# Expert outputs added to the residual by one indirect transfer of whole rows per expert, in place of three of quarter rows

## The reference, cut to what matters

```python
top_v, top_i = lax.top_k(logits, TOP_K)            # 4 of 32 experts for each of 512 tokens
top_w = jax.nn.softmax(top_v, axis=-1)
...
gu = xb @ w_gate_up[e] + b_gate_up[e]              # rows of expert e, 1024 -> 2048
gate = jnp.minimum(gu[:, :D_EXPERT], SWIGLU_LIMIT)
up = jnp.clip(gu[:, D_EXPERT:], -SWIGLU_LIMIT, SWIGLU_LIMIT)
glu = gate * jax.nn.sigmoid(SWIGLU_ALPHA * gate)
return ((up + 1.0) * glu) @ w_down[e] + b_down[e]  # 1024 -> 1024
...
y = jnp.zeros((t + 1, d), out.dtype).at[row_tok].add(out * row_w[:, None])
```

## Time and profile before

| | |
|---|---|
| median of 3 runs | 2087.03 us (2084.79 to 2087.28) |
| profiled execution: span, first to last instruction | 2083.6 us |
| TensorE busy, of the span | 2054.8 us, 99% |
| VectorE, ScalarE, GpSimd busy | 862.4, 455.5, 369.3 us |
| read from HBM, written to it | 509.09 MB, 18.88 MB |
| granted TensorE clock, mean | 0.999 |

### The profile page before, as it was taken

How to read it: one execution, slowest core, us unless ns; L and a number is a source line. 1 busy time by engine, 2 the same in 40 slices (tenths; PEclk the granted TensorE clock), 3 DMA queues, 4 the chain that set the end, 5 groups by cost and what they waited for, 6 DMA issues and landing times.

```text
span 2083.6 us, 42388 instructions
## 1 busy us (share of the span) xinstructions
PE 2054.8 (99%) x17798; PEld 1246.7 (60%) x17798; DVE 862.4 (41%) x1468; ACT 455.5 (22%) x741; POOL 369.3 (18%) x413
## 2 busy tenths in 40 slices
PE   9999999999999999999999999999999999999999
PEld 6888876344443444443443443447786788888887
DVE  4554435433333333332333332324665443444544
ACT  5151442000000000000000000024554532212211
POOL 2010001112222222222223223221202400000000
PEclk9999999999999999999999999999999999999999
DMA  7334126999999999999999999974111022323221
GB/s 263 101 122 131 61 81 254 385 400 406 408 414 407 408 413 409 408 413 406 396 412 408 408 412 404 410 257 135 61 61 41 1 81 70 112 81 101 86 102 54
DMA packets 141117, 520.14 MB, mean 250 GB/s; under 512 B 16460, under 2 KB 71936, under 8 KB 91808
## 3 DMA queue, kind: packets, MB, share of 16 engines
q1 hardware_dynamic: 120384, 495.02, 60.2%
q0 software_dynamic: 20672, 24.26, 5.0%
HBM read 509.09 MB, written 18.88 MB: 253 GB/s over the span
## 4 chain that ended last, share of the span: by engine, by line
PE 88%; DMA 7%; DVE 2%; ACT 2%; issue 1%; SPq 0%; POOL 0%; POOLq 0%; DVEq 0%; ACTq 0%
PE ps L2246 27%; PE ps L2260 13%; PE ps L395 12%; PE ps L397 12%; PE ps L396 12%; DMA ring<-in_w_gate_up 4%; DMA ring<-in_w_down 3%; PE ps L2054 1%; PE ps L2111 1%; PE ps L2141 1%; PE ps L497 1%; PE ps L1882 1%; PE ps L1903 1%; PE ps L2048 1%; PE ps L2004 1%; PE ps L2074 1%
## 5 line engine op out<-in xcount | busy, mean ns | idle before, releaser
L2246 PE MATMUL ps<-ring,xe 128*32 128x512 f32 x6144 | 668.7, 592 | 1.3 <-DMA ring<-in_w_gate_up 1.2
L2246 PEld LDWEIGHTS ps<-ring,xe 128*32 128x32 f32 x6144 | 197.1, 110 | 428.8 <-issue 405.0
L2260 PE MATMUL ps<-ring,act_t 128*32 128x256 f32 x6144 | 338.8, 379 | 3.2 <-DMA ring<-in_w_down 1.9
L2260 PEld LDWEIGHTS ps<-ring,act_t 128*32 128x32 f32 x6144 | 200.9, 110 | 148.7 <-issue 17.1
L395 PE MATMUL ps<-xt_hi,hi 128*128 128x512 f32 x544 | 213.6, 393 | 0.8 <-DVE ff_a L1734 0.8
L397 PE MATMUL ps<-xt_hi,lo 128*128 128x512 f32 x544 | 211.8, 389 | 0.0
L396 PE MATMUL ps<-xt_lo,hi 128*128 128x512 f32 x544 | 211.7, 389 | 0.0
L1139 ACT ACTIVATE glu<-glu 128x768 f32<-128x768 f32 x32 | 27.0, 844 | 635.3 <-DVE glu L1687 635.3
L789 POOL DMA_INDIRECT x_rows<-ye,idx x96 | 152.9, 1593 | 37.6 <-issue 37.6
L1654 DVE COPY idx<-idx 128x3 int32<-128x3 int32 x33 | 5.6, 169 | 352.6 <-DMA x_rows<-ye,idx 345.5
L382 DVE TENSOR_TENSOR lo<-raw,hi 128x2048 fp32r<-128x2048 f32 x44 | 101.3, 2309 | 92.2 <-ACT hi L375 85.3
(11 more groups left out here) (339 smaller groups left out, 2464.8 us busy)
## 6 DMA issues: line engine op xcount, KB each, us to landing
ring<-in_w_gate_up SPq DMA_DIRECT2D x256, 1024.0 KB, 20.9
ring<-in_w_down SPq DMA_DIRECT2D x128, 1024.0 KB, 22.6
raw<-in_w_in SPq DMA_DIRECT2D x20, 1024.0 KB, 6.3
raw<-in_w_gate SPq DMA_DIRECT2D x11, 1024.0 KB, 5.3
raw<-in_w_up SPq DMA_DIRECT2D x11, 1024.0 KB, 5.3
raw<-in_w_down SPq DMA_DIRECT2D x11, 1024.0 KB, 4.9
raw<-in_w_out SPq DMA_DIRECT2D x8, 1024.0 KB, 5.1
raw<-in_w_k SPq DMA_DIRECT2D x4, 1024.0 KB, 5.0
```

What stands on the lines that cost most here:

```text
L2246: last = pe.matmul(ps[QUAD * j:QUAD * j + QUAD, g, :], xe[:, g, QUAD * k:QUAD * k + QUAD], w[:, j, :, :], start=k == 0, stop=k == KT - 1)
L2260: last = pe.matmul(y_block(g, j, bank), act_t[:, g, QUAD * (2 * c + h):QUAD * (2 * c + h) + QUAD], w[:, h, QF * j:QF * j + QF], start=c == ...
```

## The change

Four things change together. ACT writes each quarter of a group to its own columns, so that `ye` becomes 96 partitions x 1024, one whole row of 4 KB for each slot, in twelve pieces of 32 x 256. POOL issues one accumulating transfer of these 96 rows. For it the slots' token numbers are needed once more, as one number for each of 96 partitions (`y_row`): PE makes them with three more small matmuls in `slot_sums`, and DVE with one more small instruction in `indices`. And the slots are dealt out differently: column c of the row of constants holds place (c mod 6) x 16 + c // 6, so that the tokens of an expert with fewer than 96 are spread over all slots, and not packed at the front.

```diff
-    c[:, C_SLOT:C_SLOT + P] = p[None, :]
+    place = np.arange(CAP)
+    c[:, C_SLOT + 6 * (place % 16) + place // 16] = place[None, :]
...
-        ye = at("ye", K(24), [P, GROUPS, QF])
+        ye = at("ye", K(32), [CAP, D])
...
-        idx = [at(f"idx{i}", small_i(3 + i), [P, GROUPS], I32) for i in range(3)]
+        idx = at("idx", small_i(3), [P, GROUPS], I32)
+        y_row = [at(f"y_row{i}", small_i(11 + i), [CAP, 1], I32) for i in range(3)]
...
-        x_dram = nc.dram_tensor("x_rows", [SEQ * 4, QF], F32, kind="Internal").ap()
+        x_dram = nc.dram_tensor("x_rows", [SEQ, D], F32, kind="Internal").ap()
...
         def scatter(pool, n, k, rows):
 
             pool.wait_ge(m_y, n + 2)
             hold(pool, k)
-            for g in range(GROUPS):
-                pool.indirect_dma_start(x_dram, bass.IndirectOffsetOnAxis(ap=rows[:, g:g + 1].bitcast(U32), axis=0),
-                                        ye[:, g, :], None, bounds_check=SEQ * 4 - 1,
-                                        oob_is_err=False, compute_op=ALU.add).then_inc(m_scat, 16)
+            pool.indirect_dma_start(x_dram, bass.IndirectOffsetOnAxis(ap=rows[:, :].bitcast(U32), axis=0),
+                                    ye[:, :], None, bounds_check=SEQ - 1,
+                                    oob_is_err=False, compute_op=ALU.add).then_inc(m_scat, 16)
...
                 for g in range(GROUPS):
-                    i = act.activation(ye[:, g, :], ps[:, bank + g // 2, QF * (g % 2):QF * (g % 2) + QF], ACT.Copy,
-                                       scale=w[:, g:g + 1])
+                    for j in range(4):
+                        quad = slice(QUAD * j, QUAD * j + QUAD)
+                        i = act.activation(ye[QUAD * g:QUAD * g + QUAD, QF * j:QF * j + QF],
+                                           ps[quad, bank + g // 2, QF * (g % 2):QF * (g % 2) + QF], ACT.Copy,
+                                           scale=w[quad, g:g + 1])
...
-                dve.tensor_copy(idx[2][:, :], idx[1][:, :])
+                dve.tensor_copy(y_row[2][:, :], y_row[1][:, :])
                 link(dve.tensor_copy(slot_w[:, :], slot_s[:, 1, :]))
-                dve.tensor_copy(idx[1][:, :], idx[0][:, :])
+                dve.tensor_copy(y_row[1][:, :], y_row[0][:, :])
                 link(dve.tensor_copy(slot_s[:, 0:parts, :].rearrange("p a g -> p (a g)"), ps[:, 6, 0:parts * GROUPS]))
+                dve.tensor_scalar(y_row[0][:, :], ps[0:CAP, 6, 2 * GROUPS:2 * GROUPS + 1], float(CAP), None, ALU.subtract)
...
+                for g in range(GROUPS):
+                    last = pe.matmul(ps[QUAD * g:QUAD * g + QUAD, 6, 2 * GROUPS:2 * GROUPS + 1], cc(C_OWN + QUAD * g, QUAD),
+                                     own_q[:, g:g + 1], start=True, stop=True)
                 last.then_inc(m_pos, 1)
```

More of the change, by code:

```diff
@@ L563, in x_tile_rows @@
         def x_tile_rows(t):
-            r = 4 * t * P
-            return x_dram[r:r + 4 * P, :].rearrange("(s j) c -> s (j c)", j=4)
+            return x_dram[t * P:(t + 1) * P, :]
         def moe_src(e, j):
@@ L627, in moe_loads @@
                 load_chunk(sp, SB, c)
-            sp.wait_ge(m_scat, n1 * 48 + 64)
+            sp.wait_ge(m_scat, n1 * 16 + 32)
         def f_slot(q):
@@ L780, in gather @@
             for g in range(GROUPS):
-                pool.indirect_dma_start(xg[:, g, :], None, h_dram, bass.IndirectOffsetOnAxis(ap=idx[0][:, g:g + 1].bitcast(U32), axis=0),
+                pool.indirect_dma_start(xg[:, g, :], None, h_dram, bass.IndirectOffsetOnAxis(ap=idx[:, g:g + 1].bitcast(U32), axis=0),
                                         bounds_check=SEQ * 4 - 1, oob_is_err=False).then_inc(m_gathered, 16)
@@ L804, in moe_moves @@
                 gather(pool, i + 2, i * 2 + 2)
-                scatter(pool, i, i * 2 + 3, idx[2])
-            scatter(pool, n1, n1 * 2 + 2, idx[1])
+                scatter(pool, i, i * 2 + 3, y_row[2])
+            scatter(pool, n1, n1 * 2 + 2, y_row[1])
         def scalar_program(act):
@@ L1158, in moe_scalar @@
                 act.wait_ge(m_used, i * 12 + 20)
-                y_evacuate(i * 48 + 16, i + 3, slot_w)
+                y_evacuate(i * 16 + 16, i + 3, slot_w)
             act.wait_ge(m_used, n1 * 12 + 12)
-            y_evacuate(n1 * 48 + 16, n1 + 2, slot_s[:, 1, :], 5)
+            y_evacuate(n1 * 16 + 16, n1 + 2, slot_s[:, 1, :], 5)
         def f_split_hi(act, q0, used, count, j=None):
@@ L1364, in vector_program @@
             link(dve.tensor_scalar(tiny[:, 45:46], tiny[:, 44:45], LAMBDA_INIT, None, ALU.subtract))
-            dve.wait_ge(m_scat, n1 * 48 + 64)
+            dve.wait_ge(m_scat, n1 * 16 + 32)
             lo_part(dve, SB, 0)
@@ L1653, in indices @@
                     dve.wait_ge(m_gathered, gathered)
-                dve.tensor_copy(idx[2][:, :], idx[1][:, :])
+                dve.tensor_copy(y_row[2][:, :], y_row[1][:, :])
                 link(dve.tensor_copy(slot_w[:, :], slot_s[:, 1, :]))
-                dve.tensor_copy(idx[1][:, :], idx[0][:, :])
+                dve.tensor_copy(y_row[1][:, :], y_row[0][:, :])
                 link(dve.tensor_copy(slot_s[:, 0:parts, :].rearrange("p a g -> p (a g)"), ps[:, 6, 0:parts * GROUPS]))
+                dve.tensor_scalar(y_row[0][:, :], ps[0:CAP, 6, 2 * GROUPS:2 * GROUPS + 1], float(CAP), None, ALU.subtract)
                 link(dve.tensor_scalar(row_f[:, :], slot_s[:, 0, :], 4.0, cc(C_QUAD, 1), ALU.mult, ALU.add))
-                dve.tensor_scalar(idx[0][:, :], row_f[:, :], 4.0 * CAP, None, ALU.subtract).then_inc(m_idx, 1)
+                dve.tensor_scalar(idx[:, :], row_f[:, :], 4.0 * CAP, None, ALU.subtract).then_inc(m_idx, 1)
             def pick_row(n, used):
@@ L1694, in swiglu @@
                 dve.scalar_tensor_tensor(act_e[:, :, :], glu[:, :, :], SILU_TOP, up1[:, :, :], ALU.min, ALU.mult).then_inc(m_act, 1)
-            link(dve.memset(idx[0][:, :], 0))
-            link(dve.memset(idx[1][:, :], 0))
+            link(dve.memset(y_row[0][:, :], 0))
+            link(dve.memset(y_row[1][:, :], 0))
             link(dve.memset(slot_s[:, :, :], 0.0))
@@ L1718, in moe_vector @@
                 select(i + 2, i + 1)
-                indices(i + 2, i * 48 + 16, i * 48 + 96)
+                indices(i + 2, i * 16 + 16, i * 48 + 96)
                 swiglu(i + 1, i * 12 + 16)
```

## The result

The changed kernel takes 2096.8 us (median of 4 runs, 2096.1 to 2098.1), the kernel before 2087.16 beside it (4 runs, 2084.8 to 2090.7). The ratio is 1.0042, 95% interval 1.003 to 1.0054: 9.6 us slower, where 2.1 us faster was forecast and 2082.0 to 2090.6 was the range. The profiled execution took 2096.32 us with a span of 2094.6 (before 2083.6).

The account below looks back on a forecast made before the run. PE was taken to bound the kernel nearly everywhere, the ring of weight loads late in the expert stage. Terms -6.2 + 1.9 + 1.8 + 0.4 = -2.1 us took 2087.0 to 2084.9 us, range 2082.0 to 2090.6.

Parts of the forecast that it names:

- The end of the stage: After the last expert, twelve uncovered ACT copies make PE start its next product later: +1.8 us (1.2 to 2.5).
- The rival on the slower side: Scatter rows of 4 KB at 0.5 us each delay the ring's loads: about 2100 us, chance 0.14.
- The ring's waits: In the expert loop, PE's waits for the ring of weight loads all vanish: -6.2 us.
- the ring's 1.36: In the expert loop, the DMA engines are 1.36 us per expert slower than PE, so weight loads land ever later.
- s: Time per expert saved on the DMA engines or added on PE, taken off 1.36 us; forecast 0.39 us.
- the bound of 0.23: In the expert loop, all PE waits for weight loads vanish from s = 0.23 us per expert on.
- The rival without relief: DMA time goes by bytes alone, 0.39 us per 4 KB row, relieving nothing: 2089.4 us, chance 0.16.
- PE, +1.9 us: Three added one-column matmuls per expert hold PE for 0.05 to 0.06 us, 33 times: +1.9 us.
- The rival of small matmuls that wait in their columns: The added matmuls wait for the old ones, 0.17 us per expert: 2088.5 us, chance 0.10.
- The way around the buffers: Within one expert, from copies to landed scatter: it lands at +14.7 us, 1.7 us earlier, gaining nothing as PE didn't wait.
- The start of the stage: PE's first wait for `xe` gets longer by added small instructions and a fuller gather: +0.4 us (0.1 to 0.6).

Follow-up runs that it names:

- Run 1: The changed kernel with four warm-up products on PE ahead of its wait for the last expert's copies: 2087.76 us, ratio 1.0002.
- run 3: The kernel before, with only its last expert's three copies cut in twelve of 32 partitions and its transfers kept: 2101.59 us, ratio 1.0067.
- run 9: The changed kernel with one warm-up product ahead of PE's wait for the last expert's copies: 2096.68 us, ratio 1.0022.
- Run 5: The changed kernel with the slots in plain order again, so without the new dealing: 2103.52 us, ratio 1.0072.
- run 6: The kernel before with only the three added small matmuls in each table of sums, results unread: 2088.8 us, ratio 1.0003.
- run 2: The changed kernel with the last expert's twelve copies shared between ACT and VectorE: 2084.68 us, ratio 0.9988.
- run 11: The changed kernel with the two loops of the copies exchanged: 2097.78 us, ratio 1.0039.

## Why the prediction was wrong

**The step that failed is "The end of the stage", +1.8 us (1.2 to 2.5).** It followed the late copies to PE's wait and stopped there, as if a wait cost its own length. It cost 13.6 us: 2.7 of wait, 8.2 and 2.6 of the same products at half the clock. With 13.6 in place of 1.8 the forecast's sum of -2.1 becomes +9.7, and +9.6 was measured. Run 1 shows that most of it is the clock, and run 3 that the copies alone bring it about. Both faults of the step count:
- The copies were priced at 4.5 us and took 5.73. I had taken the overlap of three large copies (1.20 us for three of 0.473) over to twelve of 32 partitions. The Trainium skill (ScalarE: Activation LUTs, "What ACT_TABLE_LOAD costs") says, of tiles of 128 partitions, that ACTIVATEs back to back overlap by about 93 ns; by that figure an estimate for twelve of 0.467 would be 4.6 us. The trace agrees for 128 partitions, with 0.1 us of overlap, and shows none for 32.
- Even the wait of 1.6 us that the step had forecast would mostly have cost the clock: run 9 has 1.69 and lost it in 9 executions of 12. Copies of 4.5 us would hardly have saved the forecast; a term for the clock was missing from it, and a rival with it.

The profile of before had no wait at this place, since PE goes from L1960 to the next product at 1392.51 with no idle time noted ahead of it. It had waits of the forecast's size elsewhere, and the two longest were followed by the full clock. The earlier one, the window behind it (granted clock 1.00), and the later one, behind which it was 1.00 too:

```profile
365.87 11.42 PE L2141 MATMUL ps<-const 128*128 128x512 f32 x26 [1.57 <-DVE n_blk L1589]
...
366.00:377.00 11.00, 11.00 (x26) 4.72 (x26) 9.79 (x43) 0.00 (x0) 3.75 (x4) 1.00 1.02 415
...
1599.63 2.42 PE L2048 MATMUL ps<-sqT,dqT 64*128 64x512 f32 x8 [2.04 <-ACT a_sb L1069]
```

But the same wait ends differently from one execution to the next. In the changed kernel's profile the earlier one was followed by half clock, and the same 26 products took 3 us longer:

```profile
363.89 14.45 PE L2145 MATMUL ps<-const 128*128 128x512 f32 x26 [1.52 <-DVE n_blk L1592]
...
364.00:370.00 6.00, 6.00 (x7) 2.40 (x8) 4.93 (x30) 0.00 (x0) 3.52 (x4) 0.50 1.00 416
```

Of the 13 profiles, all of which have both waits, 5 have half clock behind the earlier (1.52 to 1.58 us) and 11 behind the later (2.04 us), for some 3 to 7 us each time. So one profile without a loss did not show that a wait is free. Why the half clock lasted 17 to 24 us behind the wait for the copies and no more than 7 at these two places is open.

The rival on the slower side, an accumulate of 4 KB dearer than four of 1 KB, had the sign and nearly the time, and was wrong in its cause: a row takes 0.33 us. In the scatter's stretch 601.5:605.5 of the changed kernel:

```profile
q0 software_dynamic: 106, 0.24, 30.8%
```

30.8% of 64 engine-us are 19.7, over 0.24 MB or some 59 rows of 4 KB: 0.33 us each, where 0.31 was taken, worked out from the earlier trace rows. For the rival 0.5 was needed, or 0.41 at least.

**The ring's waits, -6.2 us: right in the time, half by luck in the cause.** The waits vanished, and the engine time that the transfer saves was sized rightly (0.375 us per expert for 0.33). But the prediction took this saving off the ring's 1.36 as it stood, as if each of the 16 engines had its even share whatever the order of the places. Run 5 has the same saving and PE's part, and its s of 0.13 is no more than that of run 6, where PE's part is alone: without the dealing next to nothing reached the ring, and the bound of 0.23 would have been missed. The rival without relief, which had the rows too dear, would have been right there in its consequence. With the dealing s is 0.56 to 0.72, more than the two terms together; the prediction had no term for it. That dealing spreads an expert's filled places evenly over the 16 engines, and plain order does not, fits; it was only argued, since the trace doesn't say which engine moved a packet.

**PE, +1.9 us: right.** 0.06 us per expert in the changed kernel and in run 6. The rival of small matmuls that wait in their columns fell.

**The way around the buffers: nearly right.** In the timeline of one expert of the changed kernel:

```profile
591.09 5.74 ACT L1147 ACTIVATE ye<-ps,slot_w 32x256 f32<-32x256 f32 x12 [8.68 <-PE ps L2267]
597.74 1.50 POOL L789 DMA_INDIRECT x_rows<-ye,y_row  x1 [0.56 <-issue]
606.26 0.15 DVE L1657 COPY y_row<-y_row 96x1 int32<-96x1 int32 x1 [10.03 <-DMA x_rows<-ye,y_row]
```

The scatter has landed 15.2 us after the copies' start, against 16.4 and the 14.7 forecast. It came 0.5 us later than forecast, though the copies took 1.2 us more than forecast. As said, this gain met no waiter: within the loop the slower copies cost nothing.

**The start of the stage, +0.4 us: open.** The first copy in the loop came 1.1 us later than before. But over all profiled executions the first product of the experts lies between 376.5 and 378.7 us in the four without the new transfer and between 376.9 and 381.4 in the nine with it, and the clock fell there in some executions and not in others. A cost of 1 to 2 us on average is possible; it was not separated.

With the wait at the end of the stage taken away the rest of the sum holds: run 2 has only the loop's -4.25 and whatever the start costs, and measured 2.95 us less than the kernel before.

## What to carry to other kernels

Follow a delay up to TensorE and ask whether it makes the engine idle: where it does, add a rival in which the products behind the wait run at half speed, here for 3 to 24 us, and read the granted clock behind such waits in more than one execution. Work that hides in a loop must be priced again at the loop's last pass, where its cover is missing. A few superfluous matmuls ahead of the wait turned 9.6 us lost into none, and half of the work given to another engine turned them into 3 us gained. When an indirect transfer's rows are partly out of bounds, the order of the places can decide whether a saving on the DMA engines shortens the transfers beside it: 0.375 us per expert were saved here in either order, and only one of them moved the landings.

## What was not expected of the hardware

- A wait of 2.73 us on TensorE was followed by some 20 to 24 us at 1.2 GHz while the engine was busy, in each of the three profiles with that wait (the changed kernel twice, and run 11). Behind one of 0.83 us at the same place the profile has about 17 us of it, and by the mean clock 5 executions of 12 had it; with one of 1.69 us it was 9 of 12.
- A wait of 2.04 us elsewhere was followed by 3 to 7 us at 1.2 GHz in 11 of 13 profiles, one of 1.52 to 1.58 us in 5 of 13.
- ACT's copies of 32 partitions and 256 columns take as long as those of 128 (0.467 against 0.473 us) and follow one another every 0.48 us, where the large ones follow every 0.36.
- An accumulated row of 4 KB took 0.33 us, 3.4 times the 0.098 of one of 1 KB. Dealing the same rows out anew changed nothing in the queue's time (6.4% both times) and took 0.59 us per expert off the growth of the ring's landings.
